# Twenty of the twenty-two hidden tiles of each FFN by seven half-size products, with weight sums made by adding transfers and low weight parts on VectorE alone

## What is computed

```
def swiglu_half(x, g, w_up, w_down):
    h = rmsnorm(x, g)
    gate, up = jnp.split(h @ w_up, 2, axis=-1)
    return x + 0.5 * ((jax.nn.silu(gate) * up) @ w_down)
```

## Time and profile before

| | before |
|---|---|
| median of three runs | 3029.39 us |
| the profiled execution's own time | 3033.17 us |
| its span, first to last instruction | 3031.4 us |
| mean granted TensorE clock (1 = 2.4 GHz) | 0.989 |
| bytes moved | 271.22 MB, mean 89 GB/s |

### The profile page before, as it was taken

One profiled execution on the slowest core, in us unless ns is written; L12 is line 12 of the kernel. 1 busy time (PEld: TensorE's weight loads), 2 busy tenths in 40 slices (PEclk: granted clock), 3 DMA queues, 4 the chain that ended last, 5 costly groups with the idle time before them and its releaser, 6 DMA issues.

```text
span 3031.4 us, 65367 instructions
## 1 busy us (share of the span) xinstructions
PE 2964.1 (98%) x23664; PEld 2876.5 (95%) x23664; DVE 1602.5 (53%) x2155; ACT 786.5 (26%) x1296; POOL 1752.3 (58%) x1604
## 2 busy tenths in 40 slices
PE   7999999999999999999999999999999999999998
PEld 7999999989988999999999999999898889999998
DVE  7563665535323467364674736745353245673646
ACT  4221232031232324131241312321303323331212
POOL 5666575545543575656666665654545445766665
PEclk9999999999999999999999999999999999999999
DMA  3232232232221332222232221322312123322231
GB/s 135 79 111 87 70 127 77 67 106 68 82 70 60 106 118 100 88 86 101 74 105 84 90 98 65 125 71 66 114 63 86 63 75 112 108 89 101 80 108 68
DMA packets 115174, 271.22 MB, mean 89 GB/s; under 512 B 9240, under 2 KB 53152, under 8 KB 114720
## 3 DMA queue, kind: packets, MB, share of 16 engines
q1 hardware_dynamic: 65088, 231.76, 22.7%
q10 hardware_dynamic: 49888, 36.71, 4.0%
HBM read 249.92 MB, written 18.52 MB: 89 GB/s over the span
## 4 chain that ended last, share of the span: by engine, by line
PE 88%; DVE 6%; issue 2%; ACT 2%; POOL 1%; ACTq 0%; DMA 0%; PEld 0%; DVEq 0%; POOLq 0%
PE dense L536 64%; PE SA L584 8%; PE SB L584 6%; PE SA L712 1%; PE SA L797 1%; PE SA L698 1%; PE SA L641 1%; PE SA L781 1%; PE SB L793 1%; DVE tmp L1241 1%; DVE Hl L1246 1%; POOL Wl L484 0%; PE SA L683 0%; PE SA L784 0%; PE SA L630 0%
## 5 line engine op out<-in xcount | busy, mean ns | idle before, releaser
L482 POOL TENSOR_SCALAR Wh<-raw 128x512 fp32r<-128x512 f32 x740 | 542.5, 733 | 1037.2 <-PEq L541 935.5
L484 POOL TENSOR_TENSOR Wl<-raw,Wh 128x512 fp32r<-128x512 f32 x740 | 1021.2, 1380 | 61.7
L536 PE MATMUL dense<-Hh,Wh 128*128 128x272 f32 x3104 | 663.0, 295 | 23.6 <-DVE Hl L1232 10.1
L536 PE MATMUL dense<-Hh,Wl 128*128 128x272 f32 x3104 | 648.4, 291 | 0.0
L536 PE MATMUL dense<-Hl,Wh 128*128 128x272 f32 x3104 | 647.9, 290 | 0.0
L536 PEld LDWEIGHTS dense<-Hh,Wh 128*128 128x128 f32 x3104 | 493.7, 191 | 34.8 <-issue 17.6
L536 PEld LDWEIGHTS dense<-Hl,Wh 128*128 128x128 f32 x3104 | 494.9, 191 | 0.0
L536 PEld LDWEIGHTS dense<-Hh,Wl 128*128 128x128 f32 x3104 | 492.9, 192 | 0.0
L536 PE MATMUL dense<-Ah,Wh 128*128 128x272 f32 x1408 | 290.9, 288 | 4.7 <-DVE Al L1333 4.7
L536 PE MATMUL dense<-Ah,Wl 128*128 128x272 f32 x1408 | 289.5, 288 | 0.0
L536 PE MATMUL dense<-Al,Wh 128*128 128x272 f32 x1408 | 289.2, 287 | 0.0
(11 more groups left out here) (423 smaller groups left out, 5246.9 us busy)
## 6 DMA issues: line engine op xcount, KB each, us to landing
raw<-wst SPq DMA_DIRECT2D x336, 512.0 KB, 3.3
pair<-wst SPq DMA_DIRECT2D x80, 512.0 KB, 4.0
raw<-wst SPq DMA_DIRECT2D x32, 384.0 KB, 2.9
x_keep<-X ACTq DMA_DIRECT2D x2, 2176.0 KB, 8.3
X<-x_keep ACTq DMA_DIRECT2D x16, 272.0 KB, 3.1
sst<-st_h ACTq DMA_DIRECT2D x8, 512.0 KB, 4.5
s_h<-sst ACTq DMA_DIRECT2D x8, 512.0 KB, 3.4
sst<-st_c ACTq DMA_DIRECT2D x8, 512.0 KB, 4.0
```

The costliest lines, as they stand in the source:

```text
L482: pool.tensor_scalar(Wh[:, j, cs], raw[:, j, cs], 1.0, 0.0, ALU.mult, ALU.add).then_inc(glink, 1)
L484: pool.tensor_tensor(Wl[:, j, cs], raw[:, j, cs], f32(Wh[:, j, cs]), ALU.subtract).then_inc(glink, 1)
L536: mm = pe.matmul(dps[slot][:, a, 0:HALF], w[:, ring, w0:w0 + 128], x[:, k, a * HALF:(a + 1) * HALF], start=(k == 0 and n == 0), stop=(k == ...
```

## The change

1. **Twenty fast pairs in each FFN.** Only the first two hidden tiles stay dense. FAST goes from 10 to 20 (80 pairs in all), and in a block the pairs follow each other with nothing between: 6, 8 and 6 of them, then the 8 down tiles.
2. **The weight sums are made in HBM by transfers.** GpSimd's queue issues, for groups of 1 to 8 pairs ("chunks"), six levels of transfers into the new HBM tensor `w_sums`. Each level waits until the one before has landed. Levels 0 and 1 are two transfers each, levels 2 to 5 one each. Levels 1, 3 and 5 add to what is there (`accum_op`). They are issued in GpSimd's stream between its splits: for the first FFN inside that FFN, and for the other three in the mixers, one level after every second piece.
3. **Staging.** SP loads for each pair `first` (A11, S2, S1, A12: two transfers of 512 KB) and `second` (S3, S4, A22: 512 KB and 256 KB) where it loaded two of 512 KB. `first` and `second` have one buffer each.
4. **Low parts.** All seven of a pair are made on VectorE (DVE_LO = 7), and `weights` is gone. `q_lo` now counts seven for each pair. GpSimd's `lows` has an empty range.
5. **One pair ahead.** ScalarE's high parts and VectorE's low parts of pair n+1 are woven into the reading of pair n's products. The value and gate of a pair go to alternating buffers of `tmp`. Some signs of the sums changed.
6. **Loads of down pieces.** In each block the first two down pieces are loaded ahead of the pairs, and the others after the loads of that block's pairs and of the first two pairs of the next block.

The core of the diff:

```diff
-FAST = FF_TILES // 2 - 1
+FAST = FF_TILES - 2
+FAST_AT = (0, FF_BLOCK - 2, 2 * FF_BLOCK - 2, FAST)
+DVE_LO = 7
...
 # SP
+            def load_pair(n):
+                sp.wait_ge(q_lo, ONE + n * DVE_LO)
+                sp.sem_inc(pair_began, 1)
+                at = gate_piece(n)
+                sp.dma_start(first[:, 0:4:3, :], wst[at, :, :].rearrange("p (a c) -> p a c", a=2)).then_inc(first_in, 16)
+                sp.dma_start(first[:, S2:S1 + 1, :], w_sums[0:2, n, :, :].rearrange("s p c -> p s c")).then_inc(
+                    first_in, 16)
+                sp.wait_ge(q_lo_pool, ONE + n * (7 - DVE_LO))
+                sp.dma_start(second[:, 0:2, :], w_sums[2:4, n, :, :].rearrange("s p c -> p s c")).then_inc(second_in, 16)
+                sp.dma_start(second[:, 2, :], wst[at + 1, :, 512:1024]).then_inc(second_in, 16)
...
+                    def pairs(a, b):
+                        for n in range(n0 + a, n0 + b):
+                            if n == n0 or n in [c[0] for c in CHUNKS]:
+                                sp.wait_ge(sum_done, sums_of(n))
+                                sp.sem_inc(pair_began, 1)
+                            load_pair(n)
...
+                        for m in range(KT):
+                            if m == 2:
+                                pairs(FAST_AT[b] + 2, min(FAST_AT[b + 1] + 2, FAST))
+                            load(L * STREAM + p0 + DOWN_AT[b] + m, L * PIECES + d0 + 24 * b + 2 * nf + m, m % 2, nf * P)
...
 # GpSimd
+                if sent[0]:
+                    pool.wait_ge(sum_done, 16 * sent[0])
+                    pool.sem_inc(sum_began, 1)
+                if level == 0:
+                    pool.dma_start(W1, U_a).then_inc(sum_done, 16)
+                    pool.dma_start(W3, G_a).then_inc(sum_done, 16)
+                elif level == 1:
+                    pool.dma_start(W1, U_b, accum_op=ALU.add).then_inc(sum_done, 16)
+                    pool.dma_start(W3, U_a, accum_op=ALU.add).then_inc(sum_done, 16)
+                elif level == 2:
+                    pool.dma_start(flat(w_sums[0, n0:n1, :, :]), flat(w_sums[1, n0:n1, :, :])).then_inc(sum_done, 16)
+                elif level == 3:
+                    pool.dma_start(W2, G_a, accum_op=ALU.add).then_inc(sum_done, 16)
+                elif level == 4:
+                    pool.dma_start(flat(w_sums[3, n0:n1, :, :]), flat(w_sums[0, n0:n1, :, :])).then_inc(sum_done, 16)
+                else:
+                    pool.dma_start(W4, G_b, accum_op=ALU.add).then_inc(sum_done, 16)
...
+                for p in range(MIX_PIECES):
+                    one(MIX_P0 + p, parts=(SINGLE[p],) if p in SINGLE else (0, 1))
+                    if p % 2 and p // 2 < 6 * len(ahead):
+                        sums(*ahead[p // 12], p // 2 % 6)
...
 # TensorE, in fast
-                        if q < S3:
-                            pe.wait_ge(q_lo, ONE + n * 4 + (q + 1))
+                        if q < DVE_LO:
+                            pe.wait_ge(q_lo, ONE + n * DVE_LO + (q + 1))
...
 # ScalarE, in products
+                    act.wait_ge(prod_done, 7 + n * 7 + 1)
+                    act.activation(tmp[:, 3, 0:HALF], SA[:, 0, 0:HALF], ACT.Copy).then_inc(prod_copy, 1)
+                    if ahead:
+                        high(n + 1, A11)
+                        high(n + 1, S2)
+                    act.wait_ge(ffn_lo, f - 1)
+                    act.wait_ge(prod_done, 7 + n * 7 + 3)
...
 # VectorE, in products
+                    if ahead:
+                        low(n + 1, A11)
+                    product(2)
+                    dve.wait_ge(prod_copy, n * 2 + 1)
+                    TT(U[:, h1], SA[:, 1, h0], U[:, h0], ALU.subtract).then_inc(prod_read, 1)
+                    if ahead:
+                        low(n + 1, S2)
+                        low(n + 1, S1)
...
+                    product(7)
...
+                    TT(V[:, h0], V[:, h0], SB[:, 1, h0], ALU.subtract).then_inc(prod_read, 1)
...
+                    TT(V, V, G, ALU.mult).then_inc(pair_mid, 1)
+                    if ahead:
+                        low(n + 1, A22)
+                    hidden_lo(f, j, at)
```

More of the change, by code:

```diff
@@ L67 @@
 PIECES = FFN2_D0 + FFN_PIECES
+PAIRS = DEPTH * 2 * FAST
+SUM_DMAS = 8
 G0, G1, B2, WO = 29, 61, 85, 93
@@ L489, in _, with lows, one @@
+            def lows(n):
+                for q in range(DVE_LO, 7):
+                    pool.wait_ge(q_hi, n * 7 + (q + 1))
+                    pool.tensor_tensor(Sl[:, q, :], piece(q), f32(Sh[:, q, :]), ALU.subtract).then_inc(q_lo_pool, 1)
             for L in range(DEPTH):
[L491 to L494, removed]
+                def one(p, cols=1024, parts=(0, 1)):
+                    split(L * STREAM + p, (L * STREAM + p) // 2, p % 2, cols, parts)
@@ L496, in ffn @@
                 def ffn(p0, which):
-                    for b, nf in enumerate((FF_BLOCK, FF_BLOCK, FF_LAST)):
[L498 to L509, removed]
+                    f = L * 2 + which
@@ new lines, in ffn @@
+                    n0 = f * FAST
+                    if f == 0:
+                        one_pair, two_pairs, three_pairs, next_two, block1, block2 = chunks(0)
+                        sums(*one_pair, 0)
+                        one(p0)
+                        sums(*one_pair, 1)
+                        one(p0 + 1)
+                        for level in range(2, 6):
+                            sums(*one_pair, level)
+                        sums(*two_pairs, 0)
+                        sums(*two_pairs, 1)
+                        one(p0 + 2)
+                        sums(*two_pairs, 2)
+                        sums(*two_pairs, 3)
+                        one(p0 + 3)
+                        sums(*two_pairs, 4)
+                        sums(*two_pairs, 5)
+                        sums(*three_pairs, 0)
+                        lows(n0)
+                        sums(*three_pairs, 1)
+                    else:
+                        for t in range(4):
+                            one(p0 + t)
+                        lows(n0)
@@ L904, in ffn @@
                                 combined_hi(3)
+                                for q in range(7):
+                                    high(L * (2 * FAST) + which * FAST, q)
                             act.wait_ge(slot_free[1], ONE + use)
@@ L936, in ffn @@
+                    with act.Fori(0, (FAST_AT[b + 1] - FAST_AT[b]) // 2 - (b == 2)) as i:
+                        for j in range(2):
+                            products(i * 2, FAST_AT[b] + j, b)
+                    if b == 2:
+                        products(0, FAST - 2, b)
+                        products(0, FAST - 1, b, False)
                     if b == 0 and which == 0:
@@ L1407, in ffn @@
+                    with dve.Fori(0, (FAST_AT[b + 1] - FAST_AT[b]) // 2 - (b == 2)) as i:
+                        for j in range(2):
+                            products(i * 2, FAST_AT[b] + j, b)
+                    if b == 2:
+                        products(0, FAST - 2, b)
+                        products(0, FAST - 1, b, False)
                     if b == 0 and which == 0:
```

271 lines of the change are left out of this document (141 added, 130 removed).

## The result

The changed kernel takes 3656.58 us (median of four runs, 3653.23 to 3656.96) where the one before takes 3028.89 (also the median of four, 3025.03 to 3030.26). The ratio is 1.2072, 95% interval 1.2051 to 1.2093. I had forecast slower, 3416 us with a range of 3260 to 3600. So the sign was right, and the size was 57 us past the end of the range, 240 past the forecast.

The account below looks back on a forecast made before the run. TensorE, busy 98% of the span, was taken as the bound. 3033 profiled + 303 FFNs + 10 down tiles + 44 first-FFN sums + 30 mixer sums = 3420 us, 3416 as median; range 3260 to 3600.

Parts of the forecast that it names:

- The ring: Between fast pairs, `first` waits for the last low part and low A11 precedes reading S2: 14.9 us against 10.55 of matmuls.
- The break-even period of 11.5 us: In the up stage, the pair period at which 17 T = 196.2 and the change neither gains nor loses.
- The period: Time T from one fast pair to the next: 14.9 us without the lower clock, taken as 16.0 with it.
- the clock's: TensorE's slower stretch after each pair's idle 4.3 us, on S3, S4 and A22: raises T from 14.9 to 16.0 us.
- the longer of my two cases: 6.8 us at 1.2 GHz, as after the idle 3.31 us, in each pair: T = 17.0 us.
- the lower clock is the rule: Rival, chance 0.15: each pair's idle 4.3 us brings as long a 1.2 GHz stretch as at 30 us; T = 17.0, 3484 us.
- The first and the last pair of an FFN: Up stage: each block's first pair, prepared during down tiles, takes 10.55 us; the up stage has 17 turns of T in all.
- The block edges: Down tiles: third down piece, behind loads of two next-block pairs, comes at 13.4 us, wanted at 12.0; eight times 1.3 is 10 us.
- The sums in the first FFN: GpSimd's levels, 3.5 us each for one or two pairs, delay splits and pair loads: 44 us, bounds 10 and 150.
- The sums in the mixers: Only level 1, at half rate, is over its time; some 10 us lost three times: 30 us, bounds nothing and 260.
- The rival with GpSimd blocked: Chance 0.17: GpSimd's stream waits for each level, mixer weights wait for it; adding at a quarter of copying rate, 3646 us.
- The low part's price: On VectorE, each of a pair's seven low parts takes 0.684 us; at 1.435, T would be 5.3 us longer.

Follow-up runs that it names:

- the run with early loads: Changed kernel, but SP loads `first` once the four low parts that read it are made and `second` once all seven are: 3233.35 us, 1.0678 to the kernel before.
- the filled run: Changed kernel plus 32 matmuls of 240 columns that nobody reads, in each pair ahead of S3: 3586.99 us, 1.1842 to the kernel before.

## Why the prediction was right in sign and wrong in size

- **The ring: right.** The steps I had put down (a load that waits for the last of seven, the opening low part ahead of the read that S3 needs) are the ones in the trace, and the run with early loads removes them and 423 us at once. The break-even period of 11.5 us and the sign follow from it.
- **The period: the failing step.** I had 14.9 us without the clock and took 16.0 "between the two". It is 17.1 in the pair shown and 17.0 at the median. The term that failed is the clock's: I took 1.1 us, and it is 2.3, near the 2.1 that I had for the longer of my two cases. My own row pointed there: the idle time was nearest to the 3.31 us that was followed by 6.8 us at the lower level, and I averaged it with a shorter case. The rest of the sum came out (14.8 in the filled run), in part by luck: `first` took 5.3 us where I had 4.5, and VectorE's own steps 8.8 (11.0, of which it waits 2.2 for products) where I had 9.5. 16 turns by 1.0 us and four FFNs are 64 us. The rival "the lower clock is the rule" came in with its period of 17.0 us, and I had given it 0.15.
- **The first and the last pair of an FFN.** I had taken 10.55 us for the first pair, as if down tiles stood ahead of it. None stand there, and it took 16.7 to 17.9, 26 us in four FFNs. I had counted a full turn for the last pair, behind which no other is prepared, and it took what its matmuls take: 23 us too many, which hid a part of the misses.
- **The block edges.** I had put the third down piece 1.3 us late. The edge cost 7.5, eight times: 50 us over. The load of `raw` behind the 1.75 MB of pair loads landed 8.1 us after its issue at the edge looked at (2033.6 us), where lone loads took 3.3, and TensorE's idle 3.4 to 4.6 us brought the lower clock again, which I had left out here.
- **The start of an FFN: not in the prediction.** I named the dense tiles' cover for the weights and forgot that the activation sums stood under it too. TensorE idles 6.7 us where it idled 2.6 and lost 1.7 to the clock: 10 us in four FFNs.
- **The sums in the first FFN** cost 88 us where I had 44. I had 3.5 us for a level of one or two pairs. Levels 0 and 1 of these took 8 to 9 us, TensorE idled 20.7 us for the third piece where I had 9, and SP waited 80.6 us in all, four times, for sums ahead of a pair's loads, where I had counted 4 us lost.
- **The sums in the mixers** cost 90 (63 and 27), where I had 30. The rate was not at fault: level 1 with eight pairs took 28 to 30 us in the mixers, and I had 31. GpSimd's late splits cost TensorE 21.5 and 23.0 us. That is the one harm that I had counted. The state loads were the rest in the first mixer, and the lower clock after each wait, with a granted clock of 0.94 and 0.97 where it was 0.99 and 0.98. TensorE's longest waits in the first mixer of the changed kernel:

```profile
PE dense L638 <- POOLq L520: 21.5, 3, 10.4
PE SA L730 <- DMA sst<-st_c: 17.1, 3, 7.7
PE SB L890 <- issue: 11.4, 1, 11.4
```

- **The rival with GpSimd blocked** gave 3646 us, very near to 3656, and for the wrong reason. It needed adding at a quarter of the copying rate and 260 us lost in the mixers. Adding ran at about two thirds, and the mixers lost 90 us. A total that fits is no sign that its mechanism holds.

The terms (64, 26, -23, 50, 10, 44 and 60) sum to 231 of the missing 240. They take the first FFN like the other three, and put all that it has above them to its sums. The start and the end of the launch are 3 more. The rest is rounding and the spread of the runs.

The low part's price was as I took it. The page of the changed kernel has VectorE's low parts from `first` at a mean of 685 ns:

```profile
L1453 DVE TENSOR_TENSOR Sl<-first,Sh 128x512 fp32r<-128x512 f32 x320 | 212.6, 685 | 404.2 <-ACT Sh L992 403.2
```

Beside GpSimd's work the median of one group was 1.435. In the changed kernel 15 of the 560 low parts overlap one of GpSimd's splits, with a median of 1.779 us. None of the other 545 takes over 0.694. The Trainium skill (SBUF — State Buffer, Who interferes with whom) has them dearer only while GpSimd reads SBUF, and this trace agrees. With three of the seven on GpSimd the pairs did not get longer either.

## What to carry to other kernels

When loads, conversions and reads of results go round a single buffer, write the ring down and add it up: the load must wait for the last reader of that buffer only, not for a counter that also counts later work. Where each turn leaves TensorE idle, as it did here for 3.7 us, add the lower clock to the sum as a full term (here 2.3 us of 17.1), and add it at every other new wait. Take it from the row that is nearest to the new case, not from a mean of two. And before sums are moved from an engine to transfers, price the bytes and their chain: 212 us here, to save 58 us of matmuls, most of which went to the edges.

## What was not expected of the hardware

- Work that nobody reads made the kernel 70 us faster, by keeping TensorE's clock at its upper level (granted 0.98 for 0.88 in the same FFN).
- An adding transfer from HBM to HBM took 1.5 times as long as a copy of the same size (12.0 against 8.1 us at the median for the first transfer of level 1), where I had assumed the double.
- With the sums' transfers on GpSimd's queue, the loads on ScalarE's queue came late enough for TensorE to wait 17 to 20 us for them in one mixer, with the mean DMA share of that mixer at some 0.7. Without the sums it did not wait for them.
- The same two transfers of `first`, from the same tensor, were there after 6.4 us with the loads of `second` issued right behind them, and after 5.1 us without. From the other tensors it was 5.2 and 5.1 us. The cause stays open.
